# Cross attention's scores from float32r parts of queries and keys, with two weight remainders on GpSimd

## The reference, cut to what matters

```python
def mem_cross_attention(h, mem, norm_mem_g, w_xq, w_xkv, w_xo):      # h = rms_norm(x, g)
    q = (h @ w_xq).reshape(b, s, 4, 128)                             # s = 512
    kv = (rms_norm(mem, norm_mem_g) @ w_xkv).reshape(b, m, 2, 4, 128) # m = 256
    k, v = kv[:, :, 0], kv[:, :, 1]
    logits = einsum('bqhd,bkhd->bhqk', q, k) * 128 ** -0.5
    p = softmax(logits, axis=-1)
    return einsum('bhqk,bkhd->bqhd', p, v).reshape(b, s, 512) @ w_xo
```

## Time and profile before

| | us |
|---|---|
| median of 3 runs (1764.94 to 1765.14) | 1765.05 |
| the profiled execution | 1765.09 |
| its span | 1763.3 |
| PE busy | 1754.0 (99%) |
| DVE busy | 1244.3 (71%) |
| ACT busy | 730.7 (41%) |
| POOL busy | 483.6 (27%) |

### The profile page before, as it was taken

The page is one execution under the profiler, slowest core; times in us unless marked ns, Lnnn a source line. Parts: engine busy times, 40 slices in busy tenths (PEclk is TensorE's granted clock), DMA queues, the critical chain, the costliest instruction groups (busy, mean ns, idle before and its releaser), DMA issues.

```text
span 1763.3 us, 21613 instructions
## 1 busy us (share of the span) xinstructions
PE 1754.0 (99%) x8152; PEld 1453.1 (82%) x8152; DVE 1244.3 (71%) x1656; ACT 730.7 (41%) x940; POOL 483.6 (27%) x201
## 2 busy tenths in 40 slices
PE   9999999999999999999999999999999999999998
PEld 7888888888878888888878888888888788888888
DVE  7987856563568776577779678555744797685586
ACT  5233644343464433343432346443444544343342
POOL 6453000103014244444133620010030232444440
PEclk9999999999999999999999999999999999999999
DMA  5532222322222322232332313223222223322322
GB/s 216 190 120 72 102 102 84 132 95 96 96 96 96 120 101 91 97 117 80 114 143 72 143 62 109 105 93 123 96 96 96 96 96 120 114 78 96 120 74 70
DMA packets 30120, 185.95 MB, mean 105 GB/s; under 512 B 3644, under 2 KB 5948, under 8 KB 9536
## 3 DMA queue, kind: packets, MB, share of 16 engines
q1 hardware_dynamic: 27804, 172.71, 27.6%
q0 software_dynamic: 1648, 11.54, 1.7%
q10 hardware_dynamic: 564, 0.33, 0.1%
HBM read 179.25 MB, written 7.68 MB: 106 GB/s over the span
## 4 chain that ended last, share of the span: by engine, by line
PE 98%; DVE 0%; DMA 0%; ACT 0%; issue 0%; POOL 0%; SPq 0%; DVEq 0%; ACTq 0%; POOLq 0%
PE ps L1531 28%; PE ps L1532 28%; PE ps L1541 28%; PE ps L1447 2%; PE ps L1438 2%; PE ps L1439 2%; PE ps L1569 1%; PE ps L1589 1%; PE ps L1621 1%; PE ps L1603 1%; PE ps L1581 0%; PE ps L1701 0%; PE ps L1702 0%; PE ps L1708 0%; DMA resid<-x_t 0%; PE ps L1552 0%
## 5 line engine op out<-in xcount | busy, mean ns | idle before, releaser
L1531 PE MATMUL ps<-x_hd,w_hd 128*128 128x512 f32 x1584 | 619.3, 391 | 0.0
L1532 PE MATMUL ps<-x_tl,w_hd 128*128 128x512 f32 x1584 | 616.7, 389 | 0.0
L547 POOL TENSOR_TENSOR w_tl<-raw,w_hd 128x2048 fp32r<-128x2048 f32 x80 | 370.0, 4624 | 536.1 <-ACT w_hd L652 397.3
L652 ACT ACTIVATE w_hd<-raw 128x2048 fp32r<-128x2048 f32 (+1 forms) x156 | 298.4, 1913 | 344.8 <-PE ps L1532 260.4
L1541 PE MATMUL ps<-x_hd,w_tl 128*128 128x512 f32 x1584 | 377.3, 389 | 0.0
L1531 PEld LDWEIGHTS ps<-x_hd,w_hd 128*128 128x128 f32 x1584 | 297.4, 188 | 62.7 <-issue 0.3
L1532 PEld LDWEIGHTS ps<-x_tl,w_hd 128*128 128x128 f32 x1584 | 297.4, 188 | 61.2
L1541 PEld LDWEIGHTS ps<-x_hd,w_tl 128*128 128x128 f32 x1584 | 297.0, 188 | 61.6
L1531 PE MATMUL ps<-ring_hd,w_hd 128*128 128x512 f32 (+1 forms) x640 | 242.0, 382 | 0.0
L1532 PE MATMUL ps<-ring_tl,w_hd 128*128 128x512 f32 (+1 forms) x640 | 239.8, 379 | 0.0
L900 DVE TENSOR_TENSOR w_tl<-raw,w_hd 128x2048 fp32r<-128x2048 f32 x75 | 171.9, 2293 | 51.5 <-ACT w_hd L652 40.1
(11 more groups left out here) (198 smaller groups left out, 1524.0 us busy)
## 6 DMA issues: line engine op xcount, KB each, us to landing
raw<-units SPq DMA_DIRECT2D x155, 1024.0 KB, 4.8
resid<-x_t SPq DMA_DIRECT2D x4, 512.0 KB, 8.0
bias_t<-bias_tiles POOLq DMA_DIRECT2D x8, 256.0 KB, 5.1
cg<-mem_t POOLq DMA_DIRECT2D x2, 1024.0 KB, 6.1
resid<-x_t POOLq DMA_DIRECT2D x1, 2048.0 KB, 8.3
resid_dram<-resid POOLq DMA_DIRECT2D x1, 2048.0 KB, 7.7
resid<-resid_dram POOLq DMA_DIRECT2D x1, 2048.0 KB, 8.9
out<-resid SPq DMA_DIRECT2D x7, 256.0 KB, 2.4
```

Source lines behind the costliest of these rows:

```text
L547: line.done(pool.tensor_tensor(w_tl[:, k % 2, :], raw[:, k % 2, :], w_hd[:, k % 2, :].bitcast(F32), ALU.subtract), of_unit("tail", g))
L652: line.done(act.activation(out, in_, func, **kw), *labels)
L1531: pe.matmul(dst, w_hd[:, slot, w], hd[:, src, :], start=kc == 0, stop=False)
L1532: i = pe.matmul(dst, w_hd[:, slot, w], tl[:, src, :], start=False, stop=False)
```

## The change

- **Scores.** Keys are evicted by ACT as float32r heads into `ring_hd[:, 2:4]`, and DVE makes their remainders in `ring_tl[:, 2:4]` (`key_tails`, at k = 36 behind the remainders of x, and at k = 37). Queries of heads 0 and 1 become heads by ACT (`query_heads(0)`) and remainders by DVE (`query_tails(0)`) at k = 38, in place of the two copies by DVE; those of heads 2 and 3 at k = 39: on ACT between `exps(0)` and `exps(1)`, on DVE between `normalise(0)` and `normalise(1)`. `qk` issues three float32r matmuls for each float32 one.
- **Place of the scores of heads 2 and 3.** `scores_23` stands four matmuls later, inside tile 1 of the values, ahead of kc = 2.
- **Remainders on POOL.** Those of units 41 and 42 (`CROSS_TAILS = (39, 40)`) move from DVE to POOL, between its part of the norms r1 and r2.
- **Value products.** They are issued by halves: `pv(0, 0)`, `pv(1, 0)`, then `flip(3)`, then the other six halves; the first halves wait for the values of tile 0 alone.

```diff
-BY_ACT = {"w", "v", "xk", "xv"}
+BY_ACT = {"w", "v", "xv"}
...
-POOL_TAILS = (*range(EARLY_TAILS), *range(44, 48), *range(51, NU - 4))
+CROSS_TAILS = (39, 40)
+POOL_TAILS = (*range(EARLY_TAILS), *CROSS_TAILS, *range(44, 48), *range(51, NU - 4))
...
-        kx = flat_cg[:, 0:HEADS * MEM].rearrange("p (h t) -> p h t", t=MEM)
+        kx_hd = ring_hd[:, 2:4, :].rearrange("p a (b t) -> p (a b) t", t=MEM)
+        kx_tl = ring_tl[:, 2:4, :].rearrange("p a (b t) -> p (a b) t", t=MEM)
...
-        qx = v_sb
+        qx_hd = [ring_hd[:, 0, :], ring_hd[:, 1, :], x_hd[:, 0, :], x_hd[:, 1, :]]
+        qx_tl = [ring_tl[:, 0, :], ring_tl[:, 1, :], x_tl[:, 0, :], x_tl[:, 1, :]]
...
-                for tag in ("r1", "r2"):
-                    add_squares(tag, KD - 1)
-                    power(tag, rs, ms, 4)
-                for k in POOL_TAILS[EARLY_TAILS:]:
+                add_squares("r1", KD - 1)
+                power("r1", rs, ms, 4)
+                for k in CROSS_TAILS:
+                    pool_tail(k)
+                add_squares("r2", KD - 1)
+                power("r2", rs, ms, 4)
+                for k in POOL_TAILS[EARLY_TAILS + len(CROSS_TAILS):]:
                     pool_tail(k)
...
+            def query_heads(h0, e):
+                for i in range(2):
+                    op(qx_hd[h0 + i], ps[:, banks(e) + i, :], labels=(f"xq_head{h0 + i}",), needs=(f"e{e}",))
...
                         elif kind == "xk":
-                            op(kx[:, 2 * arg:2 * arg + 2, :], ps[:, b:b + 2, 0:MEM], labels=(f"ev{e}",),
-                               needs=("mem_tail7",))
+                            op(kx_hd[:, 2 * arg:2 * arg + 2, :], ps[:, b:b + 2, 0:MEM], labels=(f"kx_head{arg}",))
+                        elif kind == "xq" and arg == 0:
+                            next_head(k)
+                            query_heads(0, e)
...
                     if k == 39:
                         next_head(k)
                         exps(0)
+                        query_heads(2, ENTRY_OF["xq", 1])
                         exps(1)
...
+            def key_tails(n):
+                e, a = ENTRY_OF["xk", n], slice(2 * n, 2 * n + 2)
+                tail(kx_tl[:, a, :], ps[:, banks(e):banks(e) + 2, 0:MEM], kx_hd[:, a, :], f"ev{e}", (f"kx_head{n}",))
+
+            def query_tails(h0):
+                e = ENTRY_OF["xq", h0 // 2]
+                for i in range(2):
+                    tail(qx_tl[h0 + i], ps[:, banks(e) + i, :], qx_hd[h0 + i], f"ev{e}", (f"xq_head{h0 + i}",))
...
                     if k == 36:
                         scaled_tails("n1", "g_x", range(KD))
+                        key_tails(0)
                         mean_square("r1", ms, 4, D)
...
-                        elif kind == "xq":
-                            for i in range(2):
-                                op(lambda: dve.tensor_copy(qx[:, 2 * arg + i, :], ps[:, b + i, :]), f"ev{e}",
-                                   needs=(f"e{e}",), independent=i)
+                        elif kind == "xk" and arg:
+                            key_tails(1)
+                        elif kind == "xq" and arg == 0:
+                            query_tails(0)
...
                     if k == 39:
-                        for h in (0, 1):
-                            normalise(h)
+                        normalise(0)
+                        query_tails(2)
+                        normalise(1)
                     if k == 40:
                         for h in (2, 3):
                             cross_maxima(h)
-                        tail_of_unit(l * NU + k + 1)
                         for h in (2, 3):
                             normalise(h)
...
-                    if k in (40, 41):
+                    if k == 41:
                         tail_of_unit(l * NU + k + 2)
...
                     for kc in range(KD):
+                        if (kind, t, kc) == ("xv", 1, 2):
+                            scores_23()
                         w = w_hd[:, :, 256 * kc:256 * kc + 256]
...
-                    if kind == "xv" and t == 0:
-                        scores_23()
...
-                    i = pe.matmul(ps[:, X_SCORES[h][qb // 2], MEM * (qb % 2):MEM * (qb % 2) + MEM],
-                                  qx[:, h, P * qb:P * qb + P], kx[:, h, :], start=True, stop=True)
+                    a, dst = slice(P * qb, P * qb + P), ps[:, X_SCORES[h][qb // 2], MEM * (qb % 2):MEM * (qb % 2) + MEM]
+                    pe.matmul(dst, qx_hd[h][:, a], kx_hd[:, h, :], start=True, stop=False)
+                    pe.matmul(dst, qx_hd[h][:, a], kx_tl[:, h, :], start=False, stop=False)
+                    i = pe.matmul(dst, qx_tl[h][:, a], kx_hd[:, h, :], start=False, stop=True)
...
                     if k == 41:
+                        pv(0, 0)
+                        pv(1, 0)
                         flip(3)
-                        for h in range(HEADS):
-                            pv(h)
+                        for h, m in ((0, 1), (1, 1), (2, 0), (2, 1), (3, 0), (3, 1)):
+                            pv(h, m)
```

More of the change, by code:

```diff
@@ L782, in _ @@
                                needs=(f"act_src{arg}",), scale=0.5)
-                        if e == LAST_OF[k] and k in AFTER_EVAC and k not in (42, FIRST_DOWN):
+                        if e == LAST_OF[k] and k in AFTER_EVAC and k not in (38, 42, FIRST_DOWN):
                             next_head(k)
@@ L1600, in qk @@
                 pe.wait_ge(vector_done, line.at(f"ev{ENTRY_OF['xq', h // 2]}"))
-                pe.wait_ge(scalar_done, line.at(f"xexp{h - 2}" if h >= 2 else f"ev{ENTRY_OF['xk', 1]}"))
+                if h >= 2:
+                    pe.wait_ge(scalar_done, line.at(f"xexp{h - 2}"))
+                else:
+                    pe.wait_ge(vector_done, line.at(f"ev{ENTRY_OF['xk', 1]}"))
                 for qb in range(TB):
-                    i = pe.matmul(ps[:, X_SCORES[h][qb // 2], MEM * (qb % 2):MEM * (qb % 2) + MEM],
-                                  qx[:, h, P * qb:P * qb + P], kx[:, h, :], start=True, stop=True)
+                    a, dst = slice(P * qb, P * qb + P), ps[:, X_SCORES[h][qb // 2], MEM * (qb % 2):MEM * (qb % 2) + MEM]
+                    pe.matmul(dst, qx_hd[h][:, a], kx_hd[:, h, :], start=True, stop=False)
+                    pe.matmul(dst, qx_hd[h][:, a], kx_tl[:, h, :], start=False, stop=False)
+                    i = pe.matmul(dst, qx_tl[h][:, a], kx_hd[:, h, :], start=False, stop=True)
                 line.done(i, f"xqk{h}")
@@ L1616, in flip, with pv @@
                 line.done(i, f"xT{h}")
[L1618 to L1623, removed]
+            def pv(h, m):
+                pe.wait_ge(scalar_done, line.at(f"xat{h}", f"ev{ENTRY_OF['xv', m if h < 2 else 1]}"))
+                i = pe.matmul(ps[:, X_OUT[h], :], vx[:, m, P * h:P * h + P], atx[h][:, m, :],
+                              start=m == 0, stop=m == MB - 1)
+                if m == MB - 1:
+                    line.done(i, f"xpv{h}")
             def scores_01():
```

## The result

The changed kernel takes 1771.67 us (median of 7 runs, 1769.13 to 1772.74) against 1765.08 before (7 runs, 1764.94 to 1765.14): ratio 1.0034, 95% interval 1.0024 to 1.0044. It is slower by 6.6 us, and the interval excludes a ratio of 1. The forecast was 1768.8 with a range up to 1770.4 and a chance of 0.50 for slower; the direction is right, the time lies 1.3 us above the range. Of before the seven runs lie within 0.2 us, of after within 3.6. The profiled execution took 1771.93, its span is 1770.2.

The account below looks back on a forecast made before the run. PE's list of matmuls was taken to bound cross attention; per layer -1.15 (scores) + 3.0 (stall) + 0.05 (next wait) = +1.9 us, +3.75 in all on 1765.09, so 1768.8 us, range 1763.0 to 1770.4.

Parts of the forecast that it names:

- Part 1: Cross-attention scores on PE: 24 float32r matmuls take 2.88 us instead of 3.45 per call, saving 2.3 us in the kernel.
- the row of the keys: Earlier trace row of 16 matmuls, same weights and 256 columns, giving the 0.120 us distance taken for the float32r scores.
- Part 2: Keys, queries 0 and 1, value halves and POOL's unit 42 remainder: no added cost; that remainder ends about 0.8 us ahead.
- Part 3: Ahead of flip(0): POOL's unit 41 remainder keeps DVE's normalise(0) out until 477.9, stalling PE 3.0 us per layer.
- the pace: DVE's normalise moves 256 elements in 349 ns where line 1028 needs 479, read as two elements at a time.
- one cast that held up a copy of POOL: DVE's double-pace cast of 8.13 to 8.55; POOL's copy of 18 elements took 385 ns, one of 14 takes 186.
- Part 4: Waits after flip(0): a stall of 0 to 0.1 us ahead of the first value product; later waits keep 0.2 or more.
- The sum without the clock: Per layer -1.15 + 3.0 + 0.05 = +1.9 us, +3.75 us in all, giving 1768.8 us.
- rival C: Behind the PE gap the clock halves for 2 to 4 us, costing 1 to 2 us more per layer: 1771 to 1773; chance 0.05.
- the sign of it in the earlier trace: At the end of the span, where PE had little to do, the granted clock goes to half, 1.2 GHz.

Follow-up runs that it names:

- e5: The e4 kernel with values(0) on ACT moved between the two halves of exps(3), pv(1, 0) waiting for the end of exps(3): 1762.49 us.
- e2: The kernel before with only the remainders of units 41 and 42 moved to POOL, scores still float32: 1771.76 us.
- e4: The changed kernel with normalise(0) putting its reciprocals into PSUM and multiplying all probabilities in one tensor_tensor: 1763.35 us.
- e7: The e2 kernel with normalise(0) keeping its sums in PSUM as in e4, scores still float32: 1764.88 us.
- e3: The changed kernel with 12 unneeded matmuls of 512 columns put into PE's queue ahead of flip(0): 1768.86 us.
- e6: The changed kernel with only the scores' part: both unit remainders on DVE, scores_23 and value products in their old places: 1764.56 us.
- e1: The changed kernel with the remainder of unit 41 back on DVE behind the maxima of heads 2 and 3: 1764.55 us.

## Why the prediction was right and where it was wrong

**Part 1, the scores: right.** 2.87 us for 24 matmuls, 2.88 was taken; the row of the keys was the right one. e5 shows the saving of 2.3 us come through whole when nothing is in its way.

**Part 2, the edits at no cost: right.** No wait of PE in the changed kernel stands at the keys, at the first queries, at `xo` or at head 44. POOL's remainder of unit 42 ends at 505.03 in layer 0 and PE uses it at 505.65, 0.6 us later, where 0.8 was said.

**Part 3, the exclusion and the gap: right.** It was argued from the pace and from one cast that held up a copy of POOL; e2, e4 and e7 show it. The first `tensor_scalar` lasted 3.32 us (3.3 was said) and the gap 2.96 (3.0). The rule of the Trainium skill, page "SBUF — State Buffer", section "Who interferes with whom", holds in all of its points that this case touches: the two-port form waits for the whole of POOL's instruction, POOL came first, and an instruction with one input from SBUF and one from PSUM does not wait (1.22 us beside POOL in e4).

**Part 4, the next waits: right in sum.** A stall of 0 to 0.1 us was given ahead of the first value product. The changed kernel, held back by its clock, does not wait there; in e3 this product starts 2.07 us after the products ahead of it (492.76 - 490.69), in the changed kernel 1.92 (494.23 - 492.31), so some 0.15 us are lost where the clock stays up.

**The sum without the clock: right.** 1768.8 was forecast (twice +1.9 is +3.8 and not the +3.75 taken, which is within the rounding). e3, in which the gap is there but the clock does not fall, measures 1768.86, and the fastest run of the changed kernel 1769.13.

**What failed is the step that left the clock out of the sum.** The slow clock behind the gap, rival C, stood at nothing in the forecast and had a chance of 0.05, with the argument that matmuls run densely up to the gap and from its end on. That argument is refuted: they do, and the clock falls all the same, in both layers of the profiled execution. C's size was right. From `flip(0)` to `flip(1)` the changed kernel takes 486.09 - 480.79 = 5.30 us in layer 0, the kernel with the filled gap 484.45 - 480.65 = 3.80:

```profile
480.65 1.09 PE L1642 MATMUL ps<-ident,merged 128*128 128x128 f32 x8
484.45 1.03 PE L1642 MATMUL ps<-ident,merged 128*128 128x128 f32 x8
```

That is 1.5 us in layer 0, where 1 to 2 a layer were given, and in layer 1 it is (1360.87 - 1355.51) - (1357.96 - 1354.15) = 1.55. C's time was 1771 to 1773, and 1771.67 was measured. So the account is -2.3 for the scores, 2 x 2.96 = +5.9 for the gaps and 2 x 1.5 = +3.0 for the clock, +6.6 in all; in the profiled execution, whose span is 6.9 longer than before, the late start adds the other 0.3. The prediction had the sign of it in the earlier trace rows and named the mechanism. What it set against it, that dense work on both sides of a gap holds the clock up, no row had shown. Once a stall of 3 us on TensorE was forecast, the term of the clock needed a chance far above 0.05, and the range had to reach 1773.

**The spread of the runs** fits this: the mean clock of the runs goes from 0.999 in that of 1769.13 over 0.998 (1769.98, 1770.17) to 0.997 and 0.996 (1771.67 to 1772.74). The profiled execution, 1771.93 at 0.997, is the one in which both falls are seen. In e2 the profiled execution shows one fall for two gaps. What decides in a given execution whether the clock falls is not settled by these runs.

**What the change is worth.** Alone its parts give little: the scores 0.5 us (e6), the remainders on POOL nothing at best (e7). Together, once the exclusion is out of the way, they give 1.7 us (e4) and with the values earlier 2.6 (e5), because the scores make PE come earlier to a remainder that POOL has ready by then and DVE, at its old place for it, has not (e1). Whether DVE could make it at an earlier place was not tried.

## What to carry to other kernels

Before work is given to GpSimd, list what VectorE does in those microseconds and in which form. In this kernel an instruction that reads two tensors from SBUF (4.50 us instead of 0.69), or one in the double pace (3.32 instead of 0.35), waits until the GpSimd instruction that began before it is through; the same arithmetic with one operand in PSUM does not. And a wait of 2 us or more on a busy TensorE can cost more than its length: price the half clock behind it with the wait, and look at the spread of the runs, which here was a sign of it.

## What the runs showed of the hardware that was not expected

- A gap of 2.25 to 2.96 us between dense matmuls can bring the granted clock from 2.4 to 1.2 GHz for 3.4 us of work behind it, 0.2 to 1.1 us after that work has begun; 1.5 to 1.7 us are lost each time. It fell behind both gaps of 2.96 in the changed kernel and behind one of the two gaps of 2.25 in e2, and behind none of the gaps of 0.9 (e6) and 1.1 us (e1). Matmuls with no use, put into the gap, avoid it (e3).
- Four `tensor_scalar` of 128 x 256 at double pace take 1.14 us, one `tensor_tensor` over the same 1024 elements with the sums broadcast from PSUM 1.22 at single pace: the form that does not exclude GpSimd costs 0.08 us more.
